# Expert blocks of a routed MoE in pairs: one set of send-back matmuls for two blocks, and expert weights as one 16 KB stretch per partition

## The reference, cut to what matters

```python
scores = sigmoid(h @ w_router)                    # 320 x 16
idx = top-2 inside the best group; wts = scores[idx] / sum
# per expert e, for the tokens that chose it:
act = silu(xb @ w_gate[e]) * (xb @ w_up[e])       # 2048 -> 1024
y   = act @ w_down[e]                             # 1024 -> 2048
out[token] += wts * y                             # summed over the two experts
x = x + gt_m * out ;  y = rmsnorm(x) * final_g
```

## Time and profile before

| | |
|---|---|
| Three timed runs | 2084.47, 2084.46 and 2076.31 us, median 2084.46 us |
| The profiled execution | 2076.4 us, its span (first to last instruction) 2074.8 us |
| TensorE busy | 1912.3 us, 92% of the span |
| VectorE, ScalarE, GpSimd busy | 593.2, 306.4, 453.4 us |
| Moved by transfers | 573.8 MB, mean 277 GB/s |
| Mean granted TensorE clock | 0.968 of full speed |

### The profile page before, as it was taken

How to read it: one execution, slowest core, us unless ns; L and a number is a source line. 1 busy time by engine, 2 the same in 40 slices (tenths; PEclk the granted TensorE clock), 3 DMA queues, 4 the chain that set the end, 5 groups by cost and what they waited for, 6 DMA issues and landing times. The chain is left out here.

```text
span 2074.8 us, 27843 instructions
## 1 busy us (share of the span) xinstructions
PE 1912.3 (92%) x10685; PEld 979.8 (47%) x10685; DVE 593.2 (29%) x1326; ACT 306.4 (15%) x690; POOL 453.4 (22%) x585
## 2 busy tenths in 40 slices
PE   4579999999999986999699999999999999999996
PEld 2137665555555544776343344433444434444333
DVE  2152144445434543012312121222122222222213
ACT  2001122212221222001300011100011000111002
POOL 0020012112211221100003322233222332223333
PEclk9679999999999998999799999999999999999998
DMA  9894365546654652754089999999999999999992
GB/s 307 305 307 113 90 201 167 176 157 191 186 153 166 182 170 61 234 160 143 1 342 414 413 410 397 392 390 404 397 394 393 392 403 391 396 397 390 403 393 84
DMA packets 248447, 573.80 MB, mean 277 GB/s; under 512 B 10691, under 2 KB 114461, under 8 KB 230899
## 3 DMA queue, kind: packets, MB, share of 16 engines
q1 hardware_dynamic: 244574, 563.76, 73.8%
q0 software_dynamic: 3200, 6.20, 1.3%
q10 hardware_dynamic: 631, 3.27, 0.6%
HBM read 567.78 MB, written 5.65 MB: 276 GB/s over the span
## 5 line engine op out<-in xcount | busy, mean ns | idle before, releaser
L1761 PE MATMUL PS<-ring,xt 128*64 128x512 f32 x2048 | 523.9, 600 | 2.0 <-DVE xt L1873 1.4
L1963 POOL TENSOR_TENSOR x<-x,tmp 128x512 f32<-128x512 f32 (+1 forms) x192 | 244.7, 1276 | 721.6 <-DVE tmp L1882 721.6
L1882 DVE TENSOR_TENSOR tmp<-PS,catT 128x512 f32<-128x512 f32 (+1 forms) x192 | 132.2, 689 | 620.8 <-PE PS L1749 616.6
L1761 PEld LDWEIGHTS PS<-ring,xt 128*64 128x64 f32 x2048 | 166.8, 136 | 294.2 <-issue 275.2
L1793 PE MATMUL PS<-ring,att 128*64 128x512 f32 x1024 | 226.7, 592 | 0.0
L698 PE MATMUL PS<-ring 128*128 128x320 f32 x672 | 223.1, 457 | 0.0
L1749 PE MATMUL PS<-catT,pwt 128*128 128x512 f32 (+1 forms) x384 | 209.9, 629 | 4.6 <-DVE tmp L1882 2.7
L1793 PEld LDWEIGHTS PS<-ring,att 128*64 128x64 f32 x1024 | 139.4, 137 | 74.5
L364 PE MATMUL PS<-ring,silT 128*32 128x512 f32 x768 | 107.7, 685 | 41.7 <-DMA ring<-in_w_ada 39.5
L698 PEld LDWEIGHTS PS<-ring 128*128 128x128 f32 x672 | 116.5, 191 | 49.3 <-issue 12.9
L1419 PE MATMUL PS<-catT,ring 128*128 128x320 f32 x512 | 138.5, 432 | 0.0
(11 more groups left out here) (409 smaller groups left out, 1649.8 us busy)
## 6 DMA issues: line engine op xcount, KB each, us to landing
ring<-in_w_gate SPq DMA_DIRECT2D x64, 2048.0 KB, 9.5
ring<-in_w_up SPq DMA_DIRECT2D x64, 2048.0 KB, 13.6
ring<-in_w_down SPq DMA_DIRECT2D x64, 2048.0 KB, 12.1
ring<-in_w_ada SPq DMA_DIRECT2D x48, 2048.0 KB, 9.1
ring<-in_w_in SPq DMA_DIRECT2D x34, 1024.0 KB, 5.8
ring<-in_w_out SPq DMA_DIRECT2D x16, 1024.0 KB, 6.0
x_a<-in_x_prompt ACTq DMA_DIRECT2D x2, 1024.0 KB, 8.2
sraw<-in_state_wkv POOLq DMA_DIRECT2D x8, 256.0 KB, 3.7
```

The costliest lines, as they stand in the source:

```text
L1761: m = nc.tensor.matmul(PS[C * g:C * g + C, c, :], xt[:, 4 * q + k, :], unit(2 * q + g, FE)[:, k, 512 * c:512 * c + 512], start=(q == 0 and ...
L1882: nc.vector.tensor_tensor(tmp[0:n_, r % 2, :], PS[0:n_, 2 + r % 2, :], gtm[0:n_, i // 2, 512 * c:512 * c + 512], ALU.mult).then_inc(sc_ev, 1)
L1963: nc.gpsimd.tensor_tensor(xx, xx, tmp[0:n_, r % 2, :], ALU.add).then_inc(x_ok, 1)
```

## The change

The blocks are worked in pairs. The even block of a pair (h = 0) writes its y and its weighted one-hot into partitions 0 to 63, the odd block (h = 1) into 64 to 127, and one set of 12 send-back matmuls then contracts over both. `ysb` becomes a tile of its own with four quarters, and `pwt` loses its zero layer and its memset. If the number of blocks were odd, one empty block would be added. The send-backs run in the gate and up part of the first block of a pair alone; VectorE's and GpSimd's 12 steps go with them. The weights are read with another assignment of input rows to partitions, `"e (q p k) n -> e q p (k n)"`: partition p takes four (or two) rows that follow each other, 16 KB in one stretch. To match it, the transposes take every fourth column of `xs` and every second of `sgt`.

```diff
-    w_gate = A["w_gate"][0].rearrange("e (q k p) n -> e q p k n", q=4, p=P)
+    w_gate = A["w_gate"][0].rearrange("e (q p k) n -> e q p (k n)", q=4, p=P)
     (w_up and w_down alike)
-        eng.dma_start(unit(u, src.shape[2]), src).then_inc(ld_e[u % 6], 16)
+        eng.dma_start(ring[:, (u % 6) * UNIT:(u % 6 + 1) * UNIT], src.rearrange("e p n -> p (e n)")).then_inc(ld_e[u % 6], 16)
...
+            o.did(tt(odd[:, :], bnum[:, 0:32:2], nb[0:1, 1, NE - 1:NE].broadcast_to([1, 16]), ALU.is_lt))
+            o.did(nc.vector.tensor_reduce(npair[:, 1:2], odd[:, :], AX.X, ALU.add))
+            o.did(ts(npair[:, 0:1], npair[:, 1:2], 2.0, None, ALU.mult))
-            o.did(nc.vector.tensor_copy(bei[:, 32:33], nb[0:1, 1, NE - 1:NE]))
+            o.did(nc.vector.tensor_copy(bei[:, 32:34], npair[:, :]))
...
-                        m = nc.tensor.transpose(PS[:, 6 + q, m_ * P:(m_ + 1) * P], xs[:, q, m_ * P:(m_ + 1) * P],
+                        m = nc.tensor.transpose(PS[:, 6 + q, m_ * P:(m_ + 1) * P], xs[:, q, m_:512:4], ident[:, :])
...
-                nc.tensor.matmul(PS[0:n_, 2 + r % 2, :], pwt[:, c % 2, t0:t0 + n_], ysb[:, c // 2, :], start=True,
+                nc.tensor.matmul(PS[0:n_, 2 + r % 2, :], pwt[:, t0:t0 + n_], ysb[:, c, :], start=True,
...
-            def experts(b):
+            def experts(j, h):
+                b = j * 2 + h
...
-                        if 1 <= 4 * q + k <= NBK and not isinstance(b, int):
-                            send_back(b, 4 * q + k - 1)
+                        if 1 <= 4 * q + k <= NBK and h == 0 and not isinstance(j, int):
+                            send_back(j, 4 * q + k - 1)
+                if h == 1:
+                    pe.wait_ge(dn_ev, b)
                 gather(b + 1)
...
-                    m = nc.tensor.transpose(PS[:, 3, f * SLOT:(f + 1) * SLOT], sgt[:, f * P:(f + 1) * P],
+                            sgt[:, 256 * (f // 2) + f % 2:256 * (f // 2) + 256:2], ident[0:SLOT, 0:SLOT])
...
-                for h in range(2):
-                    for i in range(3):
-                        m = nc.tensor.matmul(PS[C * h:C * h + C, 2, i * P:(i + 1) * P], pw[:, 0, i, :], ident[:, :],
+                for i in range(3):
+                    m = nc.tensor.matmul(PS[side[h], 2, i * P:(i + 1) * P], pw[:, 0, i, :], ident[:, :],
...
-                for h in range(2):
-                    m = nc.scalar.copy(pwt[C * h:C * h + C, h, :], PS[C * h:C * h + C, 2, 0:T])
+                nc.scalar.copy(pwt[side[h], :], PS[side[h], 2, 0:T]).then_inc(pw_ev, 1)
                 act.wait_ge(used[11 % 6], 2 * b + 2)
                 for c in range(2):
-                    m = nc.scalar.copy(ysb[:, c, :], PS[:, 4 + c, :])
+                    m = nc.scalar.copy(ysb[side[h], c::2, :], PS[side[c], 4:6, :])
...
-            with pe.Fori(1, n) as b:
-                experts(b)
+            with pe.Fori(1, n) as j:
+                experts(j, 0)
+                experts(j, 1)
...
-            with pool.Fori(1, n) as b:
+            with pool.Fori(1, n) as j:
                 for r in range(NBK):
-                    add(b, r)
-                weights(b)
+                    add(j, r)
+                weights(j * 2)
+                weights(j * 2 + 1)
```

More of the change, by code:

```diff
@@ L1295, in phase_mix @@
     bei = sb("bei", [1, 64], I32)
+    odd, npair = sb("odd", [1, 16]), sb("npair", [1, 2])
     slotf, slotw = sb("slotf", [P, SLOT]), sb("slotw", [P, SLOT])
@@ L1303, in phase_mix @@
     gtm = cat[:, 0:2 * D].rearrange("p (v n) -> p v n", v=2)
-    ysb = cat[:, 2 * D:2 * D + 1024].rearrange("p (q n) -> p q n", q=2)
     (s_x, s_br, s_rt, o_own, p_own, t_mix, u_wo, gated, t_back, x2_ok, ss_ok, sd_ok, xn_ok, t_h, h_ev, hm_ok, t_rt,
@@ L1690, in phase_mix @@
         pw = t("pw", [P, 2, 3, SLOT])
-        pwt = t("pwt", [P, 2, T])
+        pwt = t("pwt", [P, T])
+        ysb = t("ysb", [P, 4, 512])
         tmp = t("tmp", [P, 2, 512])
@@ L1694, in phase_mix @@
         block = es.enter_context(nc.Block())
-        blocks = lambda eng: eng.value_load(bei[0:1, 32:33], min_val=NE, max_val=MAXB)
+        blocks = lambda eng: eng.value_load(bei[0:1, 32:33], min_val=NE, max_val=MAXB + 1)
+        pairs = lambda eng: eng.value_load(bei[0:1, 33:34], min_val=NE // 2, max_val=(MAXB + 1) // 2)
+        side = [slice(C * h, C * h + C) for h in range(2)]
         back = [(i, t0, n, c) for i, (t0, n) in enumerate(TILES) for c in range(4)]
@@ L1721, in _ @@
         def _(pe):
-            n = blocks(pe)
+            n = pairs(pe)
             def gather(b):
@@ L1737, in gather_turn, with send_back @@
                     for m_ in range(4):
-                        m = nc.tensor.transpose(PS[:, 6 + q, m_ * P:(m_ + 1) * P], xs[:, q, m_ * P:(m_ + 1) * P],
-                                                ident[:, :])
+                        m = nc.tensor.transpose(PS[:, 6 + q, m_ * P:(m_ + 1) * P], xs[:, q, m_:512:4], ident[:, :])
                 m.then_inc(t_xt, 1)
-            def send_back(b, r):
+            def send_back(j, r):
                 i, t0, n_, c = back[r]
                 if r == 0:
-                    pe.wait_ge(dn_ev, b)
-                    pe.wait_ge(pw_ev, b)
-                pe.wait_ge(sc_ev, NBK * b + r + 1)
-                nc.tensor.matmul(PS[0:n_, 2 + r % 2, :], pwt[:, c % 2, t0:t0 + n_], ysb[:, c // 2, :], start=True,
+                    pe.wait_ge(dn_ev, j * 2)
+                    pe.wait_ge(pw_ev, j * 2)
+                pe.wait_ge(sc_ev, NBK * j + r + 1)
+                nc.tensor.matmul(PS[0:n_, 2 + r % 2, :], pwt[:, t0:t0 + n_], ysb[:, c, :], start=True,
                                  stop=True).then_inc(t_sc, 1)
-            def experts(b):
+            def experts(j, h):
+                b = j * 2 + h
                 pe.wait_ge(xt_ev, b + 1)
@@ L1778, in experts @@
                 pe.wait_ge(pw_ok, b + 1)
-                pe.wait_ge(sc_ev, NBK * b + NBK + 2)
+                pe.wait_ge(sc_ev, NBK * j + NBK + 2)
                 pe.sem_inc(past_pe, 1)
-                for h in range(2):
-                    for i in range(3):
-                        m = nc.tensor.matmul(PS[C * h:C * h + C, 2, i * P:(i + 1) * P], pw[:, 0, i, :], ident[:, :],
-                                             start=(i == 0), stop=(i == 2), skip_group_check=True)
+                for i in range(3):
+                    m = nc.tensor.matmul(PS[side[h], 2, i * P:(i + 1) * P], pw[:, 0, i, :], ident[:, :],
+                                         start=(i == 0), stop=(i == 2), skip_group_check=True)
                 m.then_inc(t_pw, 1)
@@ L1801, in _ @@
             gather_turn(0)
-            experts(0)
-            with pe.Fori(1, n) as b:
-                experts(b)
+            experts(0, 0)
+            experts(0, 1)
+            with pe.Fori(1, n) as j:
+                experts(j, 0)
+                experts(j, 1)
             for r in range(NBK):
@@ L1809, in _ @@
         def _(act):
-            n = blocks(act)
+            n = pairs(act)
             def gather_out(b):
@@ L1826, in experts @@
                 act.wait_ge(t_pw, b + 1)
-                act.wait_ge(t_sc, NBK * b + NBK)
-                for h in range(2):
-                    m = nc.scalar.copy(pwt[C * h:C * h + C, h, :], PS[C * h:C * h + C, 2, 0:T])
-                m.then_inc(pw_ev, 1)
+                act.wait_ge(t_sc, NBK * j + NBK)
+                nc.scalar.copy(pwt[side[h], :], PS[side[h], 2, 0:T]).then_inc(pw_ev, 1)
                 act.wait_ge(used[11 % 6], 2 * b + 2)
                 for c in range(2):
-                    m = nc.scalar.copy(ysb[:, c, :], PS[:, 4 + c, :])
+                    m = nc.scalar.copy(ysb[side[h], c::2, :], PS[side[c], 4:6, :])
                 m.then_inc(dn_ev, 1)
             gather_out(0)
[L1837 to L1840, removed]
+            experts(0, 0)
+            experts(0, 1)
+            with act.Fori(1, n) as j:
+                experts(j, 0)
+                experts(j, 1)
             for r, (i, t0, n_, c) in enumerate(back):
@@ L1852, in _ @@
         def _(ve):
-            n = blocks(ve)
+            n = pairs(ve)
             def picks(b):
@@ L1883, in gated, with experts @@
                                         gtm[0:n_, i // 2, 512 * c:512 * c + 512], ALU.mult).then_inc(sc_ev, 1)
-            def experts(b):
+            def experts(j, h):
+                b = j * 2 + h
                 picks(b + 1)
-                if not isinstance(b, int):
+                if h == 0 and not isinstance(j, int):
                     for r in range(NBK):
-                        gated(b, r)
+                        gated(j, r)
                 ve.wait_ge(up_ev, 2 * b + 1)
@@ L1901, in _ @@
             picks(0)
-            nc.vector.memset(pwt[:, :, :], 0.0).then_inc(pz, 1)
             turned(0)
-            experts(0)
-            with ve.Fori(1, n) as b:
-                experts(b)
+            experts(0, 0)
+            experts(0, 1)
+            with ve.Fori(1, n) as j:
+                experts(j, 0)
```

(11 more changed lines are left out.)

11 lines of the change are left out of this document (5 added, 6 removed).

## The result

The changed kernel takes 2006.74 us (median of four runs, 2004.38 to 2018.53) against 2080.39 us for the kernel before (four runs, 2074.91 to 2084.47). The ratio is 0.967 with a 95% interval of 0.964 to 0.970: 3.3% faster. The profiled execution took 2006.03 us, its span is 2004.5 us.

The account below looks back on a forecast made before the run. TensorE was taken as the bound, the transfers close behind. 72 + 5.4 - 1.0 (`ysb` copies) - 0.4 (routing) = 76 us off 2076.4 gives 2000, plus 6 for the spread of runs: 2006 us, range 1988 to 2045.

Parts of the forecast that it names:

- The bound now and the next one: Expert stage: TensorE bounds by 3.2 us per block; after the change transfers at 116.5 us per pair against TensorE's 114.1.
- Send-backs at 13.2 us: TensorE, gate and up part: eight 128-wide and four 64-wide send-backs cost 13.2 us per block; halving saves 106 us.
- TensorE's 114.1 us per pair: TensorE's need per pair: 2 x 63.67 - 13.2; line 1783 saves 0.5 us per block, strided loads cost 0.5.
- 16 KB at 432 GB/s: Weight transfers: some 10 ns fixed per stretch, so 16 KB stretches move at 432 GB/s, a pair in 116.5 us.
- 117.0 us per pair: Expert stage: transfers' 116.5 us plus 0.5 for a queue running dry; before 127.3, 72 us saved over seven pairs.
- Block 1: Block 1 loses its send-backs and runs at the transfers' rate, 58.3 us, saving 5.4.
- The copies of `ysb`: Two copies instead of one, 0.95 us more: covered in the loop, exposed behind the last block, +1.0 us.
- The long stretch without a rate: Rival, weight transfers: the long stretch brings no rate, the pairs alone act; about 43 us less, 2039 us; 17%.
- Dear strided loads: Rival, transposes: 3.3 us for `xs`, some for `sgt`; TensorE bounds again at about 120 us per pair; 2033 us; 9%.
- Transfers that keep up with TensorE: Rival, expert stage: transfers match TensorE's 114.1 us, which needs 441 GB/s; about 99 us less, 1983 us; 5%.
- Slower by the pattern of reading: Rival, weight transfers: reads farther apart break the rate; below 395 GB/s slower than before, at 360 GB/s 2177 us; 7%.
- A lower clock: Rival: TensorE, waiting in odd blocks, is granted a lower clock; at 0.79 a pair takes 144 us, some 2195 us; 3%.

Follow-up runs that it names:

- layout_only: The kernel before with 16 KB stretches and strided transposes but without the pairs; 2080.17 us against 2075.68, ratio 1.002.
- no_send: The changed kernel without the 84 send-backs, scalings and adds inside the loop; 2005.09 us against 2006.74.
- half_bytes: The changed kernel, loading only the first half of every weight unit from block 1 on, all matmuls kept; 1970.16 us.
- far: The changed kernel with the 16 KB stretches of neighbouring partitions 64 KB apart instead of 16 KB; 2009.61 us, ratio 0.967.
- the two stride kernels: The changed kernel with contiguous transposes, 2000.46 us, and with stride 8 for `xs` and 4 for `sgt`, 2007.27 us; single runs.
- pairs_only: Blocks in pairs, but weights read as before (4 KB and 8 KB stretches) and transposes contiguous; 2038.42 us, ratio 0.982 to the kernel before.
- stretch_8k: The changed kernel with all weights in 8 KB stretches and transposes to match; 2021.96 us, ratio 0.972 to the kernel before.

## Why the prediction was right, point by point

**The bound now and the next one.** Right, and shown from both sides: `layout_only` for the kernel before, `no_send` and `half_bytes` for the changed one. TensorE's own waits told what the rates hid. The waits of SP's transfers, which I took for a second proof, don't tell: they fill 88% of the time before and 89% after, although the bound has changed. I read them as a sign of transfers that follow; SP waits for a place all the same when the queue is the bound.

**Send-backs at 13.2 us.** Right. Even and odd blocks of `half_bytes` differ by 63.55 - 50.44 = 13.1 us.

**TensorE's 114.1 us per pair.** Measured 114.0. Two small terms in it were wrong and cancelled. Line 1783 gave 0.26 us per block (63.67 to 63.41, contiguous), not 0.5: I took half of the busy time, but its last records lie among the down matmuls, and from its start to the down matmuls that follow each other without it pass 0.98 us before and 0.71 after. The strided loads cost 0.14 us, not 0.5: half of them fill the wait for ScalarE, of which the rows showed 0.5 us per block, and I priced them as if nothing hid them. `layout_only`, where I used 0.9 us per block, shows the error plainly: 0.15.

**16 KB at 432 GB/s.** 428, 0.9% short, 1.1 us per pair. The fixed cost per stretch was about right (10 ns, now 9); the basis wasn't. I took it from a 7 us stretch at 426 GB/s for 8 KB, while 120 us of an always fed queue with 8 KB show 422. A short stretch, cut where a rate looked steady, overstates.

**117.0 us per pair.** 117.8 over seven pairs, 117.5 over the first six. The mean rate of 428 GB/s gives 117.6 by itself, so the miss is the rate. The 0.5 us for a queue that runs dry can't be told apart in it: the mean of 428 holds such moments already, such as 407 GB/s between 1434 and 1448 us, the end of an even block. It isn't the clock: `no_send` has four times as many stretches at the low clock and its pairs take 117.5 us, too.

**Block 1.** Predicted 58.3, measured 58.9; again the rate. In `far` and the two stride kernels it took 60.3 to 60.6 us, so its own spread is larger than that difference. Before, it had lasted 64.5 us, not 63.67, from copy to copy.

**The copies of `ysb`.** In the loop they were covered: TensorE waited for them once, behind the last block [the waits above]. There the two copies take 2.03 us instead of 1.07. But from the last copy to the end 2.2 us were added, not 1.0. The rest lies in the final chain, where ScalarE waited 9.8 us for GpSimd's adds, before 7.0, and 2.7 us for VectorE, before 4.2. From the last copy to the end it varied between kernels with the same code there, from 31.0 us (`pairs_only`) to 32.7 (`stretch_8k`), and what makes it vary was not settled; so I don't call it an effect of the change.

**The sum.** I expected 76 us less than the profiled execution and got 70.4. The pairs saved 67.0 us instead of 72, block 1 5.6 instead of 5.4, and the end cost 2.2 instead of 1.0. For the routing I took 0.4; all that lies ahead of the end of block 0 came out 0.1 us longer, which is too little to be told from the spread there. That the time itself, 2006, fell on the forecast owes something to luck. I had added 6 us because two of three runs stood at 2084.5. In 20 further runs of the kernel before the medians were 2075.7 (13 runs) and 2077.8 us (7 runs), so the allowance was not justified, and it offset the 5.6 us that I had promised too much. The time up to the end of block 0 varies by itself: it was 1084.9, 1088.0 and 1088.6 us in `no_send`, `half_bytes` and the changed kernel, which are the same up to there, and 1084.2 to 1092.4 over all kernels here.

**The rivals.** The long stretch without a rate would have been `pairs_only`: 2038 us, where I wrote 2039. It didn't happen, but its price was right: I wrote 43 us less, and the profiled executions differ by 43. (That the time fits too has the same 6 us in it as the forecast.) Dear strided loads: shown wrong. Transfers that keep up with TensorE: no, 428 is under the 441 they would need. Slower by the pattern of reading: shown wrong up to 64 KB. A lower clock: it does happen, in a small way. The price that I gave it doesn't come out of my own terms: with 144 us per pair the sum is about 2201 us, not 2195.

## What to carry to other kernels

When an engine is the bound by a few per cent only, find the next bound and its rate before pricing the gain: some 105 us of TensorE's work were worth about 40 alone and 70 with a change that by itself was worth nothing. A change that brings nothing alone may be half of a good pair, so measure it again behind the one that moves the bound. The waits of SP for places looked the same under either bound here; the waits of TensorE told them apart. Price small edits on the bounding engine against the waits that stand behind them in its own order, and take rates from long stretches in which the queue is never dry.

## What the runs showed of the hardware that I had not expected

**A stride of two is as dear as one of four.** The stationary load of a float32 transpose of `xs` takes 141 ns contiguous, 209 with stride 2, 209 with stride 4 and 193 with stride 8 (the means above), and that of `sgt` shows the same step. By the Trainium skill, page "SBUF — State Buffer", section "Specifications (TRN2)", full rate needs two hits in a line of 16 bytes; stride 2 has them and was slow all the same. The trace doesn't agree with the rule for this load. The estimate in the prediction, half the rate and 1.1 us more for the eight of `xs`, was too dear as well: at stride 4 the eight loads together are 0.55 us longer, and the block is 0.14 us longer.

**A wait of 2.7 us can be followed by the low clock.** In the changed kernel TensorE's granted clock dips where it had been waiting for weights. Stretches of the odd block from 1328.63 us:

```profile
1348.00:1352.00 4.00, 1.77 (x10) 0.37 (x5) 0.00 (x0) 0.00 (x0) 0.00 (x0) 1.00 1.00 426
1352.00:1354.00 2.00, 1.54 (x6) 0.58 (x8) 0.00 (x0) 0.00 (x0) 0.00 (x0) 0.86 1.02 434
1354.00:1356.00 2.00, 2.00 (x8) 0.81 (x6) 0.00 (x0) 0.00 (x0) 0.00 (x0) 0.50 1.02 434
1356.00:1358.00 2.00, 2.00 (x9) 0.72 (x8) 0.00 (x0) 0.00 (x0) 0.00 (x0) 0.78 0.98 418
```

In the middle the groups of matmuls are 0.85 us apart instead of 0.43, as their loads show (start us, us):

```profile
1353.34 0.18 PEld L1766 LDWEIGHTS PS<-ring,xt 128*64 128x64 f32 x2 [0.26 <-issue]
1354.08 0.30 PEld L1766 LDWEIGHTS PS<-ring,xt 128*64 128x64 f32 x2 [0.55 <-issue]
1354.93 0.30 PEld L1766 LDWEIGHTS PS<-ring,xt 128*64 128x64 f32 x2 [0.56 <-issue]
...
1357.18 0.17 PEld L1766 LDWEIGHTS PS<-ring,xt 128*64 128x64 f32 x2 [0.26 <-issue]
```

This is the 1.2 GHz level, 0.50 of full clock. But the wait alone doesn't decide it. Here is the last quarter of the gate and up matmuls in two odd blocks, each behind a wait of 2.7 us:

```profile
1235.00 7.09 PE L1766 MATMUL PS<-ring,xt 128*64 128x512 f32 x32 [2.71 <-DMA ring<-in_w_up]
1352.46 8.78 PE L1766 MATMUL PS<-ring,xt 128*64 128x512 f32 x32 [2.69 <-DMA ring<-in_w_up]
```

The first ran at a granted clock of 1.00 throughout, the second lost 1.7 us. The first's stretch where the second fell:

```profile
1236.00:1238.00 2.00, 2.00 (x12) 0.75 (x10) 0.00 (x0) 0.00 (x0) 0.00 (x0) 1.00 1.02 434
```

Of the changed kernel's six waits of 2.7 us, four were followed by the low clock and two were not; what decides between them, no run here shows. From the end of block 0 to that of block 15, TensorE never waited longer than 0.6 us in the kernel before, `layout_only` and `half_bytes`, and there was no dip at all.

The odd blocks differ by this. Without a wait of 2.7 us they last 52.3 or 52.5 us, with one 53.9 or 54.0, with one and a dip 55.6 or 55.7. The kernel as a whole hardly pays for it, since TensorE has 3.5 us to spare in each pair: `no_send` lost 1.7 us to the low clock sixteen times, and its pairs took the same 117.5 us. Whether the time would hold with less slack was not tried.
